# Banked endings for token-major products, a reordered mLSTM, an earlier first norm and a rearranged attention projection

## The reference

```python
hx = rms_norm(x, norm1_g[layer]) * (1 + mod_x[1]) + mod_x[0]       # hc alike, of the context
q, k, v, o, g, gb, gc, u = jnp.split(h @ w_in, splits, axis=-1)     # layer 0: v is used token-major
...
s = jnp.einsum('bhcjd,bhcsd->bhcjs', q, k) * d                      # mLSTM, per chunk
num = jnp.einsum('bhcjs,bhcsv->bhcjv', s, v) + a[..., None] * jnp.einsum('bhcvd,bhcjd->bhcjv', c0, q)
den = jnp.sum(s, axis=-1) + a * jnp.einsum('bhcd,bhcjd->bhcj', n0, q)
h = num / jnp.maximum(jnp.abs(den), jnp.exp(-m))[..., None]
...
hn = rms_norm(h_forward + h_backward, mnorm_g)                      # per head
m_out = hn * jax.nn.sigmoid(o)
...
qx = apply_axial_rope(rms_norm(heads(px[..., :nq], ATT_HEADS), q_g), cos, sin)   # layer 1; kx alike
kx, vx = kv(px[..., nq:])
```

## Time and profile before

| | before |
|---|---|
| median of 3 runs | 2734.12 us (2724.08 to 2736.72) |
| the profiled execution, its own time | 2727.04 us |
| its span | 2725.3 us |
| busy PE, DVE, ACT, POOL | 2449.7, 1515.5, 953.8, 1121.6 us |
| mean granted clock of TensorE | 0.945 of full |

### The profile page before, as it was taken

One profiled execution on the slowest core, in us unless ns is written; L12 is line 12 of the kernel. 1 busy time (PEld: TensorE's weight loads), 2 busy tenths in 40 slices (PEclk: granted clock), 3 DMA queues, 4 the chain that ended last, 5 costly groups with the idle time before them and its releaser, 6 DMA issues.

```text
span 2725.3 us, 31892 instructions
## 1 busy us (share of the span) xinstructions
PE 2449.7 (90%) x11622; PEld 1979.2 (73%) x11622; DVE 1515.5 (56%) x2033; ACT 953.8 (35%) x1491; POOL 1121.6 (41%) x843
## 2 busy tenths in 40 slices
PE   6999769899999997769989999898798888899999
PEld 5888657788888886546668888676544565688887
DVE  6756756755555543988651222369578534452533
ACT  3312221512121224547652332353343343432322
POOL 1433003344444431347634557345454231344444
PEclk6999879899999998979989999899899899999999
DMA  5323103233333331231123332232300120232323
GB/s 226 116 95 130 47 1 121 88 103 113 109 107 115 103 114 39 82 71 41 45 72 100 100 92 92 77 101 79 114 1 0 44 73 16 84 95 92 100 93 108
DMA packets 68823, 231.69 MB, mean 85 GB/s; under 512 B 8049, under 2 KB 10993, under 8 KB 68593
## 3 DMA queue, kind: packets, MB, share of 16 engines
q1 hardware_dynamic: 68720, 230.35, 26.4%
HBM read 219.57 MB, written 2.10 MB: 81 GB/s over the span
## 4 chain that ended last, share of the span: by engine, by line
PE 72%; DVE 13%; issue 7%; POOL 4%; ACT 3%; DMA 0%; SPq 0%; POOLq 0%; DVEq 0%; ACTq 0%
PE PS L649 51%; PE PS L667 9%; POOL HL L519 4%; PE PS L686 2%; DVE RD L2276 2%; PE PS L618 1%; PE PS L1086 1%; PE PS L910 1%; DVE SM L2260 1%; PE PS L1179 1%; PE PS L1075 1%; DVE STATE L2115 1%; PE PS L792 0%; PE PS L795 0%; DMA EARLY<-adastream 0%
## 5 line engine op out<-in xcount | busy, mean ns | idle before, releaser
L519 POOL TENSOR_TENSOR HL<-RAW,HL 128x512 fp32r<-128x512 f32 x614 | 900.9, 1489 | 1454.7 <-ACT HL L1224 1454.5
L649 PE MATMUL PS<-HA,HL 128*128 128x512 f32 (+1 forms) x2592 | 555.9, 367 | 17.4 <-DVE V L2041 5.1
L649 PE MATMUL PS<-HID,HL 128*128 128x512 f32 (+1 forms) x2832 | 561.8, 360 | 0.0
L649 PE MATMUL PS<-HB,HL 128*128 128x512 f32 (+1 forms) x2592 | 540.0, 360 | 0.0
L649 PEld LDWEIGHTS PS<-HID,HL 128*128 128x128 f32 x2832 | 478.3, 188 | 81.9
L649 PEld LDWEIGHTS PS<-HA,HL 128*128 128x128 f32 x2592 | 445.5, 191 | 108.1 <-issue 31.5
L1224 ACT ACTIVATE HL<-RAW 128x1024 fp32r<-128x1024 f32 x307 | 323.2, 1053 | 498.7 <-PE PS L649 381.2
L649 PEld LDWEIGHTS PS<-HB,HL 128*128 128x128 f32 x2592 | 442.5, 189 | 75.0
L1893 DVE CUSTOM_DVE_ANT_0 ADJ<-ADA,CB 128x1024 f32<-128x1024 f32 x160 | 265.3, 1658 | 8.4 <-DVE X L1815 2.7
L1815 DVE SCALAR_TENSOR_TENSOR X<-PS,MOD,X 128x256 f32<-128x256 f32 (+1 forms) x120 | 75.8, 659 | 330.3 <-PE PS L649 312.2
L667 PE MATMUL PS<-HA,HL 128*128 128x256 f32 (+1 forms) x576 | 137.5, 402 | 61.5 <-DVE HA L1796 49.2
(11 more groups left out here) (372 smaller groups left out, 2744.7 us busy)
## 6 DMA issues: line engine op xcount, KB each, us to landing
RAW<-wstream SPq DMA_DIRECT2D x307, 512.0 KB, 3.5
ADA<-adastream SPq DMA_DIRECT2D x80, 512.0 KB, 3.7
EARLY<-adastream SPq DMA_DIRECT2D x16, 512.0 KB, 14.2
QB<-QH SPq DMA_DIRECT2D x32, 128.0 KB, 2.3
X<-x_in SPq DMA_DIRECT2D x8, 384.0 KB, 6.5
QC<-QL SPq DMA_DIRECT2D x16, 128.0 KB, 2.3
out<-X SPq DMA_DIRECT2D x8, 256.0 KB, 2.2
X<-mem SPq DMA_DIRECT2D x1, 1024.0 KB, 13.3
```

What stands on the lines that cost most here:

```text
L519: a = pool.tensor_tensor(HL[:, t % RING, 1, half], RAW[:, t % RAW_RING, half], HL[:, t % RING, 0, half].bitcast(F32), ALU.subtract)
L649: mm = pe.matmul(bank(t % 2, r), w[:, wp, k * P:(k + 1) * P], a[:, ap, lo:hi], start=(k == 0 and (wp, ap) == (0, 0)), stop=(k == nk - 1 an ...
```

## The change

1. Startup: PE takes 9 chunks and DVE 7 (ADA_PE). Chunks i and 9 + i are loaded next to each other and counted in groups of two such pairs. `norm_sum` comes after PE's second chunk, the first norm's root and the first two scalings after DVE's second; the norm's loop no longer makes its root, and ACT splits weight tile 2 inside that loop.
2. `gemm_wide`: if the tile before isn't token-major, it waits only for the tile before that one, does banks that are surely free first and waits for the others before their first product. In its last tile the banks are outermost, each with a signal, and DVE copies each bank as it ends. In the last tile all `ready(k)` waits come first.
3. mLSTM: PE signals `summed` after the numerators and makes the state's sums after that (`state_sums`); KW is made by POOL; DVE does the inverse and the second half before the state; the norm's multiply is four ACT copies with a scale.
4. Attention projection: the first newton operation becomes a Square on ACT; the constants and the high half of v are written by ACT (`values_high`, `fixed`), the low half of v by DVE ahead of the jobs; scratch moves to X's context columns, so `mem` is loaded after the queries' moves; `weights(T_OUT1 + 2)` to `(T_OUT1 + 4)` are issued behind the 20 key moves.
5. Semaphores of the MLPs are shared between layers.

```diff
-ADA_PE = 8
+ADA_PE = 9
...
+def early_group(j):
+
+    return min((j if j < ADA_PE else j - ADA_PE) // 2, 3)
...
-        for j in (i, ADA_PE + i):
-            load(early(j), adastream[j], f"early_in{j // 4}")
+        for j in (i, ADA_PE + i)[:1 + (ADA_PE + i < ADA_FIRST)]:
+            load(early(j), adastream[j], f"early_in{early_group(j)}")
...
-    stretch(t, T_OUT1 + RING + 1)
-
-    sp.wait_ge(S("norm_scaled"), of_norm("1a", "scaled", KC))
-    load(X[:, :, 0:NCTX], mem, "mem_in")
+    stretch(t, T_OUT1 + 2)
...
+    stretch(T_OUT1 + 2, T_OUT1 + RING + 1)
...
+    load(X[:, :, 0:NCTX], mem, "mem_in")
...
+    lows(0, 25 + AHEAD)
+    pool.wait_ge(S("act_once"), ACT_ONCE["cols_read"])
+    pool.wait_ge(S("tile_done"), 25)
+    for n in range(N_ML):
+        if WITH_STATE[n]:
+            d, b = ML_STEPS[n]
+            if n >= 2:
+                pool.wait_ge(S("state_sums"), states_until(n - 1))
+            pool.tensor_tensor(KW[:, n % 2, :, :], KTOK[:, b, :, :],
+                               EK[:, b, d, :].unsqueeze(2).to_broadcast([P, ML_HEADS, 64]),
+                               ALU.mult).then_inc(S("k_weighted"), 1)
+    lows(25 + AHEAD, T_OUT1 + AHEAD)
...
+        order = list(zip(blocks, banks))
+        last = lambda bk: bk // 2 == (t0 - 1) % 2 and bk < 4
+        if PLAN[t0 - 1][1] == "W":
+            banks_free(t0, 0, wide=True)
+        else:
+            order.sort(key=lambda x: last(x[1]))
+            banks_free(t0, 0)
...
+            if k == 0 and last(bk) and not freed[0]:
+                banks_free(t0, 0, wide=True)
+                freed[0] = True
...
+            if j < n - 1:
+                for kk in range(per):
+                    k = (j * per + kk) % KC
+                    if ready:
+                        ready(k)
+                    for b, bk in order:
+                        mm = product(k, kk, t, b, bk)
+            else:
                 if ready:
-                    ready(k)
-                for b, bk in zip(blocks, banks):
-                    for wp, ap in ((0, 0), (0, 1), (1, 0)):
-                        mm = pe.matmul(PS[:, bk, 0:width], H(k)[:, ap, b * P:(b + 1) * P],
-                                       HL[:, t % RING, wp, kk * width:(kk + 1) * width],
-                                       start=(k == 0 and (wp, ap) == (0, 0)),
-                                       stop=(k == KC - 1 and (wp, ap) == (1, 0)))
+                    for kk in range(per):
+                        ready((j * per + kk) % KC)
+                for i, (b, bk) in enumerate(zip(blocks, banks)):
+                    for kk in range(per):
+                        mm = product((j * per + kk) % KC, kk, t, b, bk)
+                    if i < len(blocks) - 1:
+                        mm.then_inc(S("bank_done"), 1)
...
             pe.wait_ge(S("masked"), n + 1)
             if n:
                 pe.wait_ge(S("num_read"), n)
-                pe.wait_ge(S("state_new"), states_until(n))
+            if n >= 2:
+                pe.wait_ge(S("state_new"), states_until(n - 1))
             for c in range(2):
-                pair = slice(2 * c, 2 * c + 2)
                 dst = PS[:, 4 + c, 0:2 * (ML_DV + 1)]
-                values = V1[:, b, pair, :].rearrange("p h n -> p (h n)")
                 if n >= 2:
                     pe.matmul(dst, QW[:, n % 2, c, :], STATE[d][:, c, :], start=True, stop=True)
                 for i in range(2):
                     o = slice(i * (ML_DV + 1), (i + 1) * (ML_DV + 1))
                     mm = pe.matmul(dst[:, o], DT[:, n % 2, 2 * c + i, :], V1[:, b, 2 * c + i, :], start=(n < 2),
                                    stop=True, skip_group_check=(n >= 2))
-                if WITH_STATE[n]:
+            mm.then_inc(S("summed"), 1)
+            if WITH_STATE[n]:
+                pe.wait_ge(S("k_weighted"), states_until(n + 1))
+                if n:
+                    pe.wait_ge(S("state_new"), states_until(n))
+                for c in range(2):
+                    pair = slice(2 * c, 2 * c + 2)
                     mm = pe.matmul(PS[:, STATE_BANK[c], 0:2 * (ML_DV + 1)],
-                                   KW[:, n % 2, pair, :].rearrange("p h n -> p (h n)"), values, start=True, stop=True)
-            mm.then_inc(S("summed"), 1)
+                                   KW[:, n % 2, pair, :].rearrange("p h n -> p (h n)"),
+                                   V1[:, b, pair, :].rearrange("p h n -> p (h n)"), start=True, stop=True)
+                mm.then_inc(S("state_sums"), 1)
...
+        if i == 1:
+            norm_sum("0a", "cx")
...
+    gemm_wide(t, 4, 512, (2, 3, 0, 1, 4, 5), (2, 3, 0, 1, 5, 6))
...
+    norm_root("0a", "cx")
+    for t in range(2):
         high(t)
-    norm("0a", "cx", shift((0, 0)))
+    act.wait_ge(S("dve_once"), ONCE["first_gains"])
+    norm("0a", "cx", shift((0, 0)), root=False, between=lambda: high(2))
...
+    def normed(i):
+        b = ML_STEPS[DONE[i]][1]
+        act.wait_ge(S("h_root"), i + 1)
+        for h in range(ML_HEADS):
+            a = act.activation(HS[:, b, h, :], HS[:, b, h, :], ACT.Copy, scale=RT[:, i % 2, h:h + 1])
+        a.then_inc(S("h_norm"), 1)
...
+        act.wait_ge(S("hn_rsqrt"), 3 * j + 2)
+        act.activation(spans(R2[:, j % 2, 0:hi - lo]), r, ACT.Square).then_inc(S("hn_rsqrt"), 1)
+
+    def values_high():
+        act.wait_ge(S("free_V"), freed_by["V"][T_OUT1 - 10])
+        act.activation(VH[:, :, :, 64:P], const(C_ONE)[:, 0:64].unsqueeze(1).unsqueeze(1).to_broadcast([P, 6, KV_HEADS, 64]),
+                       ACT.Copy)
+        act.activation(VH[:, :, :, 0:64], VA[:, :, :].rearrange("p b (k d) -> p b k d", d=64),
+                       ACT.Copy).then_inc(S("act_once"), 1)
+
+    def fixed():
+        act.wait_ge(S("k_in"), 16 * 5 * KV_HEADS)
+        act.activation(IDR[:, :], const(C_ID), ACT.Copy)
+        act.activation(QC[64:P, :, :], const(C_ID)[64:P, 0:1].unsqueeze(1).to_broadcast([64, 3, NX]), ACT.Copy)
+        for k in range(6):
+            a = act.activation(H(k)[64:P, :, 0:256], const(C_ID)[64:P, 64:65].unsqueeze(1).to_broadcast([64, 2, 256]), ACT.Copy)
...
+        if i == 1:
+            values_high()
+        if i == SLOTS:
+            fixed()
...
+        if i == ADA_PE + 1:
+            norm_root("0a", "cx")
+    modulation(0, ADA_PE, ADA_FIRST)
     modulation(0, 0, ADA_PE)
-    modulation(0, ADA_PE, ADA_FIRST)
     gains(0, 1, PC["n1g"])
-    norm("0a", "cx")
+    dve.sem_inc(S("dve_once"), 1)
+    norm("0a", "cx", root=False)
...
+    def bank_ready(base, i, n, tiles):
+
+        if i < n - 1:
+            dve.wait_ge(S("bank_done"), base + i + 1)
+        else:
+            dve.wait_ge(S("tile_done"), tiles)
...
-        dve.tensor_tensor(HS[:, b, :, :], HS[:, b, :, :], RT[:, i % 2, :].unsqueeze(2).to_broadcast([P, ML_HEADS, ML_DV]),
-                          ALU.mult).then_inc(S("h_norm"), 1)
+        dve.sem_inc(S("h_root"), 1)
...
-            state(s - 1)
             inverse(s - 1)
             if SECOND[s - 1]:
                 second_half(s - 1)
+            state(s - 1)
...
+        dve.wait_ge(S("hn_rsqrt"), 3 * j + 3)
+        r, t2 = hr(j, n), spans(R2[:, j % 2, 0:n])
+        link(dve.scalar_tensor_tensor(t2, spans(PS[:, 5 + 2 * (j % 2), 0:n]), HEAD_DIM * EPS, t2, ALU.add, ALU.mult))
+        link(dve.scalar_tensor_tensor(r, t2, 3.0 * HEAD_DIM, r, ALU.subtract, ALU.mult))
+        refined(spans(dst), spans(dst), r, HEAD_DIM).then_inc(S("hn_scaled"), 1)
```

More of the change, by code:

```diff
@@ L673, in gemm_wide, with product @@
             def gemm_wide(t0, n, width, blocks, banks, ready=None):
[L675 removed]
                 per = TILE // width
+                order = list(zip(blocks, banks))
[5 more added lines that the diff above has]
+                    banks_free(t0, 0)
+                freed = [False]
+                def product(k, kk, t, b, bk):
+                    if k == 0 and last(bk) and not freed[0]:
+                        banks_free(t0, 0, wide=True)
+                        freed[0] = True
+                    for wp, ap in ((0, 0), (0, 1), (1, 0)):
+                        mm = pe.matmul(PS[:, bk, 0:width], H(k)[:, ap, b * P:(b + 1) * P],
+                                       HL[:, t % RING, wp, kk * width:(kk + 1) * width],
+                                       start=(k == 0 and (wp, ap) == (0, 0)),
+                                       stop=(k == KC - 1 and (wp, ap) == (1, 0)))
+                    return mm
                 for j in range(n):
@@ L1259, in norm @@
                 act.activation(RS[:, lo:hi], RS[:, lo:hi], ACT.Exp, scale=-0.5).then_inc(S("norm_rsqrt"), 1)
+            def norm(n, regions, bias, root=True, between=None):
+                if root:
+                    norm_root(n, regions)
                 for k in range(KC):
+                    if k == 3 and between:
+                        between()
                     act.wait_ge(S("norm_scaled"), of_norm(n, "scaled", k + 1))
@@ L1288, in quarter @@
                         lo, hi = span(regions)
```

(14 more changed lines are left out.)

111 lines of the change are left out of this document (50 added, 61 removed).

## The result

The changed kernel took 2695.52 us, median of 4 runs (2692.87 to 2699.91), beside 2729.10 for the kernel before in the same series: a ratio of 0.9884, 95% interval 0.9860 to 0.9907, so 1.16% or some 32 us faster. Run again in a later series it gave 0.9884 once more (0.9861 to 0.9907). The prediction was 2715 with 2698 as its lower end: right in direction, but the time came out 19.5 us lower, outside the range. Of these, 5 are the base: the prediction took 18.8 off a median of 2734.12, and the kernel before stands at 2729.10 here. The other 14.5 are gain that the sum did not have. The two profiled spans differ by 34.2 us (2725.3 to 2691.1), and they show where. Each row of this table is a place that both traces have; times are starts in us.

A forecast was written before the change was run, and what follows sets the result against it. PE was taken to bound the kernel, with 72% of the chain, so gains lie where it idles or runs slow. 4.9 + 2.4 + 7 + 3.9 + 0.6 = 18.8 off the median gave 2715 us, range 2698 to 2733.

The forecast's parts named there:

- the new waits: Attention projection: value product's second tile waits for the whole norm, delay 4.8; DVE waits before job 10, behind 20 moves.
- Startup: Kernel start: PE begins on the fourth load, both sides end at 52.8; 4.9 us saved, bounds 4 to 6.
- the price of a chunk: Startup: each of PE's nine chunks was taken at 3.43 us, the price at a granted clock of 0.50.
- First product: First token-major product: free banks first cover PE's idle of 2.44, banked copies give nothing; 2.4 us, bounds 0 to 3.
- mLSTM: mLSTM steps: PE's load decides after the reordering, plain steps 4.75 for 6.22; 7 us saved, bounds 2 to 12.
- The sum of 10.6 at full clock: mLSTM: seven plain steps save 10.2, three with a transpose 0.3 each, the eleventh loses 1.3, the last wins 0.8.
- Two thirds of 10.6: mLSTM: a third of the time at half level, where PE's doubled load bounds both kernels, so 7 us remain.
- Attention layer: Attention projection: value product delayed by 4.8, jobs and end save 8.7; net 3.9 us, bounds -7.9 and 10.6 - 5.3.
- The rest: Cross-attention values save the last copy of two, 0.6, bounds 0 to 1.5; layer 2's self-attention values and shared semaphores nothing.
- Rival 2: Key moves go faster or land early, and the mLSTM's denser PE keeps full clock: gain 29, 2705 us; chance 0.18.
- Rival 4: mLSTM: KW on POOL holds up DVE by 0.94 each time, leaving a gain of 9.4, 2725 us; chance 0.07.
- Rival 5: Attention projection, SP's queue: each 1 us more per key move costs 20 us; 2.5 a move gives 2752; chance 0.07.

The follow-up runs named there:

- the filled kernels: The kernel before and the changed kernel, each with extra unread products issued on PE ahead of its mLSTM waits; ratios 0.9969 and 0.9864.
- after_again: The changed kernel itself, measured again with nothing altered, against the kernel before; ratio 0.9884.
- after_filled_short: The changed kernel with extra unread products of corrected length ahead of PE's waits in the mLSTM; ratio 0.9864 against the kernel before.

## Why the prediction fell short

The direction, the places of the waits and the new waits were right. What failed is the size of three terms, and each time by the clock, which was taken from one stretch and held fixed, or left out. The largest is the mLSTM's.

**Startup, 4.9 forecast; 8.2 in the trace, 7.4 (3.5 to 11.5) alone.** The waits were where they were put, only that DVE and not PE ended last. The failed step is the price of a chunk: "19.0 + 9 x 3.43 + 2.91" takes 3.43 for all nine from a stretch where PE stood at 0.50 behind an idle of 5.83. After the change four chunks ran at 1.9 to 2.0, the sum of squares and with it DVE's root came 3.3 earlier (27.52 for 30.8), and DVE ended 3 earlier. The level varies between executions, and the bound of 6 left that out.

**First product, 2.4 forecast; 4.1.** The idle of 2.44 went, the copies gained nothing, as said. What was missing is the slow clock behind the idle, 18.17 for 16.52. The same effect was counted in the attention layer, but not here.

**mLSTM, 7 forecast; 17.1 with the out projection, 13.9 (9.0 to 18.8) alone.** The mechanism held: with the inverse ahead of the state a plain step is PE's load, 4.5 for the 4.75 forecast, the eleventh step is 1.2 longer between the filled kernels (1.3 forecast), and `KW` costs nothing. The sum of 10.6 at full clock held too: step by step at the full level the runs give 11.4 in all, with the eleventh's loss in it: the seven plain steps 11.4 for 10.2, the three with a transpose 0.6 for 0.9, the last 0.6 for 0.8. The failed step is "Two thirds of 10.6". It holds that at the half level PE's load doubles to 9.2 and bounds both orders, so that a third of the gain is lost. Nothing was lost. PE is at the half level for a part of a step only: one that began there took 7.85 in the old order (346.71 to 354.56) and 6.71 in the new (297.55 to 304.26), 1.1 apart. And the new order stands there less, 0.85 for 0.78 over the stretch, which adds some 4.5. The prediction read 0.84 from 300 to 380 us, which leaves out the slow ends, and held it fixed, though its upper bound of 12 names "fewer gaps, more full clock". The out projection's first tiles, which no term had, gave 1.2 behind a shorter idle.

**Attention layer, 3.9 forecast; 3.9.** The mechanism was right, and both new waits are shown by their removal: the moves took 12.8 for 13.0, the attention began 101.6 behind its first key tile for 101.5. That the net agrees to the tenth is luck: -5.9 for -4.8 and 9.8 for 8.7 cancel, and in `after_again` the same way from the sum to the attention took 141.9 and not 139.0, which leaves 0.9 of the 3.9.

**The rest, 0.6; 1.2 in the trace,** within what one execution can tell.

**The rivals.** Rival 2 was nearest in size, and half right in cause: the moves were not faster and the stall was there, but its other half, a denser PE that keeps more of the full clock, holds in part, 0.85 for 0.78 and some 4.5 us. Rival 4 fell: with `KW` on GpSimd or on DVE the stretch is 90.5 and 90.6, and DVE's state, which has PSUM as an input, takes 1.44 beside GpSimd's 0.61 and 1.44 without it. The lock that the Trainium skill states (SBUF — State Buffer, section SBUF: two separate sides) is for a DVE operation with two SBUF inputs, and so this row agrees with it. Rival 5 fell at 0.64 a move.

## What to carry to other kernels

When an idle in front of PE is removed, the slow clock behind it goes too: price the work behind the idle at both levels, and put the difference into the range. Do not scale a gain at full clock down by the share of slow time: the change moves that share too. Take the clock over the very stretch that changes, and give the term a bound for either way. In a loop of several engines, look first for an operation on another engine that stands ahead of the one PE waits for; and when two steps are compared, look first whether both stand at the same level, since the first step here seemed to gain 3.5, half of it clock. A change that gains may carry new waits: two of them, found by reading where PE and DVE stood idle in its trace, and one multiply on the wrong engine were worth 17 us more.

## What was not expected of the hardware

- PE's granted clock falls in stretches of waiting and is paid for by the work behind them, even where PE is then wholly busy: the startup's chunks at 0.50 with PE busy without a gap. It can also fall amid work: in the changed kernel's startup PE is busy all the time from 18.80 to 25.3, and the clock is 1.00 until 20.7, 0.88 to 22.6 and 0.50 from there to 25.3. Products that nobody reads, issued into six norms and the mLSTM, gave 14.7 us of 2680, and the granted clock of 430 to 460 us went from 0.78 to 1.00.
- A product of 128 columns from fp32 data appears as two instructions, and costs about 0.235 us at the full level (20 of them took 4.73 in `after_filled_short`).
- The same program shows its half level at different places: the old order's stretch took 103.2 to 108.6 us in four traces, the new one 89.5 to 92.2 in six (one of them with the key weighting on DVE). A difference of 3 us between single traces of a stretch like this says nothing, unless the steps are compared at one level.
